# Copying three window caches in smaller parts, spread over each layer of a hybrid decoder kernel

## What is computed

```python
for l in range(2):
    # input projection, then three groups of heads, then output projection with a residual
    qkv, gates, conv_in = project(rms_norm(x, norm_w[l]), w_in[l])
    a = dsa_attention(...)       # an indexer scores 2048 cached keys; the best 256 are attended
    c = dilated_attention(...)   # windows of 128, 512 and 2048 over three caches
    b = ssd_branch(...)          # convolution, chunked scan, gated norm
    x = x + concat(a, c, b) @ w_out[l]
    # returned too: each window cache with its first 4 rows dropped and 4 new rows appended
    for buf, kn, vn in zip((cache_dil0, cache_dil1, cache_dil2), k_new, v_new):
        kk = concat([buf[:, :, 0], kn]); vv = concat([buf[:, :, 1], vn])
        new_buf = stack([kk[:, 4:], vv[:, 4:]])
y = rms_norm(x, final_norm_w)
```

## Time and profile before

| quantity | value |
|---|---|
| runs shown, median of 3 | 947.12 us (947.01, 947.12, 957.99) |
| the profiled execution's own time | 946.23 us |
| its span, first to last instruction | 944.4 us |
| mean granted clock of TensorE | 0.843 of full speed |
| HBM read, written | 190.80 MB, 52.00 MB |
| DMA queue of POOL (q0) | 50.82 MB, 15.7% of the 16 engines' span |
| DMA queue of SP (q1) | 133.49 MB, 42.4% |

### The profile page before, as it was taken

One profiled execution on the slowest core, in us unless ns is written; L12 is line 12 of the kernel. 1 busy time (PEld: TensorE's weight loads), 2 busy tenths in 40 slices (PEclk: granted clock), 3 DMA queues, 4 the chain that ended last, 5 costly groups with the idle time before them and its releaser, 6 DMA issues.

```text
span 944.4 us, 12592 instructions
## 1 busy us (share of the span) xinstructions
PE 780.7 (83%) x4338; PEld 543.7 (58%) x4338; DVE 372.6 (39%) x1150; ACT 155.9 (17%) x409; POOL 58.9 (6%) x84
## 2 busy tenths in 40 slices
PE   5989999989755387997989899999793647799885
PEld 3755566757544365555767455766572536556564
DVE  3234530366555710245033354114755574023432
ACT  2102111221322120101100121112114223010100
POOL 0000000010101010031000000000101111001200
PEclk8999999999955589567989999999995566965598
DMA  9327789965597448651733578897729880967221
GB/s 349 133 99 253 229 263 294 311 227 203 205 349 265 155 135 268 196 178 76 256 129 104 179 218 256 261 325 263 268 98 364 276 288 23 299 209 219 102 89 51
DMA packets 89299, 199.81 MB, mean 212 GB/s; under 512 B 10802, under 2 KB 76499, under 8 KB 82195
## 3 DMA queue, kind: packets, MB, share of 16 engines
q1 hardware_dynamic: 70130, 133.49, 42.4%
q0 software_dynamic: 2976, 50.82, 15.7%
q10 hardware_dynamic: 16128, 14.69, 5.2%
HBM read 190.80 MB, written 52.00 MB: 257 GB/s over the span
## 4 chain that ended last, share of the span: by engine, by line
PE 72%; DVE 15%; DMA 6%; ACT 4%; issue 2%; SPq 1%; ACTq 0%; DVEq 0%
PE bank L792 69%; DMA dil<-in_dil 3%; PE bank L842 3%; DMA kv<-in_vv 2%; DVE cacc L1322 1%; DVE relu L1726 1%; DVE hit L1340 1%; ACT shared L671 1%; DVE st L1531 1%; DVE rstd L1289 1%; DVE shared L1526 1%; SPq L422 1%; DVE st L1577 0%; DMA x<-in_x 0%; ACT srow L693 0%
## 5 line engine op out<-in xcount | busy, mean ns | idle before, releaser
L792 PE MATMUL bank<-xn,w 128*128 128x288 f32 x1408 | 375.7, 420 | 13.3 <-DVE xn L1292 7.1
L792 PEld LDWEIGHTS bank<-xn,w 128*128 128x128 f32 x1408 | 266.9, 194 | 95.3 <-issue 19.2
L588 ACT ACTIVATE pt<-bank 128x288 f32<-128x288 f32 x56 | 23.0, 411 | 255.2 <-PE bank L792 255.2
L792 PE MATMUL bank<-cnt,const 128*128 128x1 f32 x136 | 24.1, 248 | 48.6 <-DVE hit L1340 41.6
L792 PE MATMUL bank<-kv,sct 128*32 128x256 f32 x512 | 57.1, 521 | 8.6 <-DMA kv<-in_vv 8.6
L792 PE MATMUL bank<-kv,qz 128*32 128x512 f32 x256 | 63.9, 621 | 0.0
L792 PEld LDWEIGHTS bank<-cnt,const 128*128 128x128 f32 x136 | 27.6, 228 | 61.0 <-issue 56.8
L1304 DVE TENSOR_TENSOR tmp<-bank,const 128x288 f32<-128x288 f32 x30 | 13.7, 458 | 120.2 <-PE bank L792 120.2
L516 POOL DMA_DIRECT2D out_keep<-in_buf x48 | 23.5, 495 | 572.0 <-PE bank L792 570.6
L792 PE MATMUL bank<-dil,pt 128*32 128x128 f32 x288 | 37.4, 288 | 13.7 <-DMA dil<-in_dil 13.7
L1340 DVE TENSOR_SCALAR_CACHE_REDUCE hit<-sc,tb 128x516 bf16<-128x516 f32 x62 | 46.5, 749 | 2.2
(11 more groups left out here) (234 smaller groups left out, 856.5 us busy)
## 6 DMA issues: line engine op xcount, KB each, us to landing
w<-in_w SPq DMA_DIRECT2D x44, 1024.0 KB, 5.4
kv<-in_kk SPq DMA_DIRECT2D x256, 160.0 KB, 3.3
out_keep<-in_buf POOLq DMA_DIRECT2D x16, 2044.0 KB, 13.4
dil<-in_dil SPq DMA_DIRECT2D x32, 576.0 KB, 5.5
kv<-in_vv SPq DMA_DIRECT2D x144, 128.0 KB, 3.2
kv<-in_vv ACTq DMA_DIRECT2D x112, 128.0 KB, 3.2
out_keep<-in_buf POOLq DMA_DIRECT2D x16, 508.0 KB, 8.3
shared<-in_ssd SPq DMA_DIRECT2D x2, 1536.0 KB, 12.1
```

Source lines behind the costliest of these rows:

```text
L588: act.activation(ptile(i), src[:, 0:T], fn).then_inc(use, 1)
L792: return pe.matmul(out, lhsT, rhs, start=start, stop=stop, skip_group_check=True, **k)
```

## The change

The copy of the largest cache, 2044 KB for a sequence, is cut into four parts of 511 KB. A layer has 32 such parts; part `n` belongs to sequence `n // 4`. The first part of a sequence is accompanied by the 124 KB copy of the smallest cache and the second by the 508 KB copy of the middle one. Each part is issued behind a step of its own:

- parts 0 to 7 behind the early tiles `proj1` to `proj8`,
- parts 8 to 15 behind the late tiles `proj26`, 27, 28, 29, 31, 32, 33 and 35 (the feature stores follow part 8),
- parts 16 to 23 behind `va2`, `pa00`, `pa10`, `pd00b`, `pd10b`, `pd11b`, `ties` and `dnt`,
- parts 24 to 31 behind the output tiles `out0` to `out7`, after the stores of the state.

The bytes copied are the same. The DMAs for the copies go from 24 to 48 in a layer, and the count that POOL waits for at the end of the layer goes with them.

```diff
@@ PER @@
-    ... "h_out": 32, "copied": 16 * 24,
+    ... "h_out": 32, "copied": 16 * 48,
@@ block.gpsimd, for each layer @@
                 pool.memset(qcz, 0.0).then_inc(S["qcz_zero"], 1)
-                for b, use in enumerate((f"proj{LATE + 1}", f"proj{NTILE - 1}", "va2", "pa00", "pa10", "pd00b", "pd10b", "pd11b")):
-
+                def keep_part(n, use):
+                    b, part = n // 4, n % 4
                     pool.wait_ge(filled(use), nth(L, use))
-                    for g in range(3):
-                        pool.dma_start(a[f"keep{g}"][ly, b], a[f"buf{g}"][ly, b, 4 * 256:]).then_inc(S["copied"], 16)
-                    if b == 0:
+                    step = (WINS[2] - NQ) * 64
+                    pool.dma_start(a["keep2"][ly, b, part * step:(part + 1) * step],
+                                   a["buf2"][ly, b, 4 * 256 + part * step:4 * 256 + (part + 1) * step]).then_inc(S["copied"], 16)
+                    if part < 2:
+                        pool.dma_start(a[f"keep{part}"][ly, b], a[f"buf{part}"][ly, b, 4 * 256:]).then_inc(S["copied"], 16)
+
+                for n in range(8):
+                    keep_part(n, f"proj{n + 1}")
+                for n, use in enumerate([f"proj{LATE + k}" for k in (1, 2, 3, 4, 6, 7, 8, 10)] + ["va2", "pa00", "pa10", "pd00b", "pd10b", "pd11b", "ties", "dnt"]):
+                    keep_part(8 + n, use)
+                    if n == 0:
...
                 pool.dma_start(a["s_ssd"][ly].rearrange("o p a n -> (o p) a n"), state[:, :, :]).then_inc(S["h_out"], 16)
+                for m in range(KT):
+                    keep_part(24 + m, f"out{m}")
...
-                pool.wait_ge(S["copied"], nth(L, "copied", 16 * 24))
+                pool.wait_ge(S["copied"], nth(L, "copied", 16 * 48))
```

More of the change, by code:

```diff
@@ L23 @@
 DEPTH = 2
+WINS = (128, 512, 2048)
 D_MODEL = 1024
@@ L228 @@
     "y_ready": 3, "ysq": 3, "mix_b": 1, "xwb_ready": 8, "kv_used": 59, "dil_used": 14,
-    "feat_out": 48, "state_in": 16, "tail_out": 16, "h_out": 32, "copied": 16 * 24,
+    "feat_out": 48, "state_in": 16, "tail_out": 16, "h_out": 32, "copied": 16 * 48,
     "w_in0": 176, "w_in1": 176, "dil_in0": 128, "dil_in1": 128,
@@ L1866, in laid_out @@
     return {k: T_(y) for k, y in out.items()}
-WINS = (128, 512, 2048)
 OUTS = {"y": (P, KT, T), "feat": (DEPTH, P, 11, T), "tails": (DEPTH, P, NXBC, 27), "p_ssd": (DEPTH, P, 384),
```

## The result

The changed kernel takes 962.96 us (median of four, 959.91 to 966.14), against 947.66 for the kernel before on the same chip. The ratio is 1.0155, with a 95% interval of 1.0109 to 1.0202. The forecast was 953.0 and the range ended at 961.0: the kernel is slower, as forecast, but by some 15 us where 6 were expected. Two more measurements of it came later, under the labels e10 and e4; they gave 1.0074 and 1.0107, with the intervals shown there. By the medians the three put the loss at 15, 8 and 10 us.

The account below looks back on a forecast made before the run. PE was taken to bound the kernel, transfers mattering only where it waits. Terms 0 + 0 + 0 + 5.9 us on the profiled 946.2 gave 952.1, and the median's 0.9 more gave 953.0; range 946.0 to 961.0.

Parts of the forecast that it names:

- The frame: Whole kernel: PE is busy for 83% of the span, so a transfer matters only where PE waits for it.
- Output tiles: Load for `out4`, both layers: copies delay it 2.0 to 3.4 us, hidden by 3.4 us slack; at worst 1.8 us.
- what has reached the engines goes first: DMA queues: a weight load issued 0.3 us ahead of a 124 KB copy took 4.8 us, as if alone.
- Hand-over: Layer 0 to layer 1: copies delay the next layer's first weight item, so PE waits at `proj0`; 5.9 us.
- the second rival: Hand-over: small parts fit into gaps of the load queue, so the loss stays hidden; 947.1 us, chance 0.22.
- the slack of 2.2 us: Hand-over: first weight item lands at 476.6, `proj0` starts at 478.75, leaving 2.2 us.
- In the last layer the part behind `out7` ... nothing: End of program: the last part takes 1.6 us and lands before final norm and store are done; no cost.
- That is under 2 us later for a clear that ACT needs some 25 us later: nothing: Attention stage: two parts ahead of POOL's clear of `pz` delay it under 2 us; no cost.
- the attention stage keeps its 96 us: Attention stage: a sign of the forecast, its length stays at 96 us in the changed kernel.
- The third rival: Other weight loads: copies go ahead of every load, stalls of 13.1 to 16.3 us; 960 to 963, chance 0.16.
- a POOL step that comes late: Place not given: part of the unnamed rest, with a stall on a page load; chance 0.05 together.
- The fourth rival: Attention stage, both layers: thinning the copy burst makes it faster, outweighing the hand-over from about 6%; chance 0.05.

Follow-up runs that it names:

- e10: The changed kernel once more, unchanged: 955.70 us, ratio 1.0074 to the kernel before.
- e4: The changed kernel with output parts described as 128 short rows, which were merged again, so in effect a repeat: 959.97 us, ratio 1.0107.
- e8: Against the changed kernel, only parts 0 to 7 stay behind the early tiles; the others, cut in quarters, go at old places: 948.69 us, 1.0023.
- e2: The changed kernel with parts 24 to 31 behind the attention steps, none behind the output tiles: 947.61 us, ratio 1.0007.
- e14: The same kernel as e2 measured again, in five rounds: 946.44 us, ratio 0.9985.
- e1: Against the changed kernel, copies cut the same way but all issued at the eight old places: 950.87 us, ratio 1.0034.
- e3: Against the changed kernel, only parts 24 to 31 stay behind the output tiles; the others are cut but at old places: 959.07 us, 1.0105.
- e15: The changed kernel with output parts in layer 1 only; in layer 0 they go behind the attention steps: 950.91 us, ratio 1.0028.
- e6: The changed kernel with the clear of `pz` ahead of the parts behind `ties` and `dnt`: 960.44 us, ratio 1.0105.
- e16: The changed kernel with parts 24 and 25 moved behind `ties` and `dnt`; parts 26 to 31 stay: 952.54 us, ratio 1.0052.
- e9: The changed kernel with output parts in layer 0 only; in layer 1 they go behind the attention steps: 957.24 us, ratio 1.0092.
- e11: The changed kernel with output parts copied through interleaved rows to get smaller packets: 972.49 us, ratio 1.0249.
- e12: The kernel before, with POOL waiting at its end for the final norm; no copy moved: 949.54 us, ratio 0.998.
- e7: The kernel before, with POOL's clear of `pz` waiting for `msk4` instead of `dnt`: 945.20 us, ratio 0.9941.
- e13: The same kernel as e7 measured again, in five rounds: 946.30 us, ratio 0.9989.

## Why the prediction came out too low

The frame held. For the early tiles (e8), and for these with the late tiles and the cut (e2, e14), no loss can be told, and e1 bounds that of the cut at 6 us; most of the loss lies in the output stage (e3 has it, e2 and e14 don't); and it is a loss. But I had looked at transfers alone: two of the four costs below come from POOL itself. Point by point:

**Output tiles: "I take 2.0 to 3.4 us, hidden; at worst 5.2 - 3.4 = 1.8 us". This step failed.** The load came 5.4 us later than alone (10.5 against 5.1), and the stall is 1.9 us in layer 0 and 2.6 in layer 1. In layer 1 it is lost time: 2.9 us in after, 2.1 to 2.5 in e3, e4, e10 and e15. I read the earlier trace rows as "what has reached the engines goes first" from one load issued 0.3 us ahead of a copy. But that copy was 124 KB. Here the load was issued at 454.57, 0.3 us ahead of part 25, and both parts of 511 KB and the 508 KB copy were in flight with it. Part 25 landed at 461.3, the 508 KB copy at 463.0, part 26 (issued 4.1 us behind the load) at 464.8, and the load at 465.1: last of all. From about 456 on, 1.05 MB of weights, 1.04 MB in part 25 and its companion and 0.52 MB in part 26 are 2.6 MB; at the 0.33 MB/us of the earlier trace rows that takes 7.9 us and ends at 464, near the 465.1. This sum of everything that is in flight or joins, and not only of what stands ahead, gives about the latest landing, and I should have set it against the slack. It is no rule for when a load lands. SP's queue, which carries the load, had moved 0.88 MB by 460, and only the last pieces of the load came after that (queue view of 454.5 to 460, packets, MB, share):

```profile
q1 hardware_dynamic: 117, 0.88, 49.2%
```

And in two profiles with the same parts at the same places, layer 0 of e4 and layer 1 of e6, the load landed ahead of the 508 KB copy and of part 26, after 7.2 and 8.2 us, and PE didn't stall. This is the first of them, from the DMA issues of 451.6 to 451.9 of e4:

```profile
w<-in_w SPq DMA_DIRECT2D x1, 1024.0 KB, 7.2
```

What decides between the two outcomes stays open. Without parts 24 and 25 (e16) the load takes 6.7 us and there is no stall.

**Hand-over: "I take 5.9 us". The mechanism held, its size was too large in the changed kernel.** The item landed 13.3 us after its issue (14.6 in e10, 12.9 in e16), not 17.0 (8.9 and 8.1 more). From `out6` to `proj0` the cost is 1.7 us in after, 3.2 in e16, and 3.5 to 4.0 in e9 and e3. But in layer 0 this can't be told apart from the stall at `out4`. From the issue of the load for `out4` to the start of `proj0` it took 30.8 us in each of the ten profiles without output parts in layer 0 and 34.7 in after. It took 34.1 in e16 and 34.6 in e4, which have no stall at `out4` there, and 36.3 to 37.1 in e3, e6, e9 and e10 (40.0 in e11, with its small packets). In all that have output parts in layer 0, `proj0` started 0.24 us behind the landing of the item. So the item ends this stretch, and a stall at `out4` falls inside it. Layer 0 lost 3.9 us in after, and 3.3 to 6.3 in the others without small packets: the 5.9 lies within that.

Two things were off. The copies did fit in part into gaps of the load queue, as the second rival said. These are the stretches from the last products of `out0` to `out4` and from there to `proj0`, in the changed kernel:

```profile
449.60:465.10 15.50, 13.60 (x48) 10.04 (x48) 1.83 (x5) 1.77 (x4) 2.93 (x6) 0.89 0.66 233
465.10:489.30 24.20, 18.97 (x76) 14.29 (x77) 6.19 (x11) 2.27 (x5) 2.90 (x6) 0.97 1.00 393
```

At a share of 1.00 the engines moved 393 GB/s, where the earlier trace rows had 351 and 266 at 1.01 and 0.92: a full share leaves room. And the 8.9 us of the earlier trace rows was a low value: in the ten profiles without output parts in layer 0 it was between 8.9 and 9.9, so part of the slack of 2.2 us was an accident of one execution.

**"In the last layer the part behind `out7` ... nothing". This step failed: 2.4 us.** The part did land early enough (954.1, the store of `y` at 960.7). I asked when the transfer ends, not what POOL does after it. POOL's DRAIN takes 8.9 us with 108 DMAs, and starts only when the last copy has landed. e12 shows the step by itself, in the kernel before. The DRAIN of before ended 45 us ahead of the end, so that its length of 4.97 us could be read in the trace but cost nothing.

**"That is under 2 us later for a clear that ACT needs some 25 us later: nothing". This step failed: 2.8 us in both layers.** I asked who reads `pz`, and not who works beside POOL while it is cleared. The two parts moved the start of the clear from 0.77 us ahead of the mask's to 0.43 us behind it, so that all of it falls into the mask. In the views of waits of the attention stage of layer 0, PE waits 2.4 us for `maskbf` before and 3.6 after. The Trainium skill (GPSIMD Engine Reference, 1. Specifications) says that GpSimd shares its interfaces to SBUF with VectorE, with contention in some modes of the latter. The traces agree that the mask is held up beside the clear: 0.30 us without the clear beside it (e2, e7), 1.1 to 2.65 with it, and the end of the mask always 0.15 to 0.16 us behind that of the clear. In which mode the mask ran no run here shows, nor why it was held in the changed kernel, where it started ahead of the clear. The same numbers bear on "the attention stage keeps its 96 us": it went up by 1.9 and 2.7, of which 1.2 and 1.5 are this; the rest is within what this stage varies in layer 0 of kernels with a mask of 1.42 us (91.2 to 93.0).

**The sum.** 3.8 us in the output stage of layer 0 (2.1 ahead of `out4`, 15.5 against the usual 13.4, and 1.7 at the hand-over), 2.9 at `out4` and `out5` of layer 1 (1.1 + 1.8), 2.4 at the end and 2.8 at the masks are 11.9 us. The three measurements of the kernel gave 15, 8 and 10. The forecast had 5.9, all in layer 0; the 8.1 us of the last three places it had put at nothing. The third rival (stalls at the other weight loads too) had the place of the `out4` stalls right, but not the early tiles, where the loads issued in the stage took 4.7 to 6.4 us and PE never waited. Its 960 to 963 takes in the first measurement, but that is luck: its sum had 7.5 us at the hand-over and 2.0 at the early tiles. The two places worth together 5.2 us that no case named were POOL's, and I had put 0.05 on "a POOL step that comes late". The fourth rival has a slip in its arithmetic: 1% of the attention stage is 1 us in each of two layers, so some 3% of it, not 6%, would outweigh the 5.9 us.

What stays open: why the first measurement (15 us) lies above the other two, since the profiled span of after has 4.5 us more in the stage of the values, which no experiment ties to the copies; and the cost of small packets.

The best versions here are e14 (parts spread over early tiles, late tiles and attention steps, none in the output stage) and e13 (the old copies, with the clear of `pz` later). At 0.9985 and 0.9989 neither can be told from the kernel before.

## What to carry to other kernels

A load that runs beside copies can land as late as all that is in flight with it or joins it: compare the whole sum of bytes with the slack, as the cautious case, and keep large copies out of stages where a load has less slack than that. When work is moved on an engine off the critical path, ask three things of it: who waits for its result, whose instructions run beside it at its new time, and what the engine still has to do after its last instruction. When two waits lie one behind the other, look at what ends the whole stretch before adding them. Here the background copies cost nothing that could be told when they stood far from the end of the program and outside the stage whose loads are awaited.

## What the runs showed of the hardware

- POOL's closing DRAIN takes 0.082 us for each DMA that POOL issued in the whole program (1.046, 4.970 and 8.890 us for 12, 60 and 108), whatever their sizes and however long ago they landed.
- A VectorE conversion of 128x516 bf16 that takes 0.30 us alone took 1.1 to 2.65 us beside a POOL clear of 128x2334 f32, and ended 0.15 to 0.16 us behind it. DMA issues of POOL beside it didn't lengthen it (0.29 us in e16).
- Copies in packets a quarter as long delayed the weight load beside them more (10.9, 13.8 and 19.4 us against 10.8, 10.6 and 14.6), though the bytes were the same. A copy of 511 KB with no load beside it landed after 5.0 us instead of 3.9.
- DMA shares of 0.92, 1.00 and 1.01 were seen at 266, 393 and 351 GB/s; a full share doesn't tell that the engines are at their limit.
